# Modulation sums as rows, and latent heads scaled by token, in a two-block transformer kernel

## What is computed

```python
m_lat = silu(c) @ w_ada + b_ada            # 6 x 2048: sh1, sc1, g1, sh2, sc2, g2
m_ctx = silu(c_ctx) @ w_ada + b_ada        # only csh1, csc1 are used
u_lat = rmsnorm(x, norm1_g) * (1 + sc1) + sh1
u_ctx = rmsnorm(ctx, norm1_g) * (1 + csc1) + csh1
p_lat, p_ctx = u_lat @ w_in, u_ctx @ w_in
# HGRN2: 8 heads of 128, chunks of 64 tokens, in both directions
o = scores(q, k) @ v + (q * exp(a)) @ state             # 256 tokens x 128 per head
o = o * rsqrt(mean(o * o, axis=-1) + EPS) * norm_g      # mean over the head's 128 features
x = x + g1 * (concat(o * silu(g), hyena(p_lat)) @ w_out)
x = x + g2 * mlp(rmsnorm(x, norm2_g) * (1 + sc2) + sh2)
```

## Time and profile before

| | us |
|---|---|
| runs, median (lowest to highest of three) | 2680.01 (2679.8 to 2683.56) |
| the profiled execution's own time | 2679.24 |
| its span | 2677.4 |
| PE matmul busy | 2642.8 (99%) |
| DVE busy | 1833.4 (68%) |
| ACT busy | 1323.8 (49%) |
| POOL busy | 281.4 (11%) |
| HBM traffic over the span | 212 GB/s |

### The profile page before, as it was taken

One profiled execution on the slowest core, in us unless ns is written; L12 is line 12 of the kernel. 1 busy time (PEld: TensorE's weight loads), 2 busy tenths in 40 slices (PEclk: granted clock), 3 DMA queues, 4 the chain that ended last, 5 costly groups with the idle time before them and its releaser, 6 DMA issues.

```text
span 2677.4 us, 42752 instructions
## 1 busy us (share of the span) xinstructions
PE 2642.8 (99%) x18168; PEld 2414.4 (90%) x18168; DVE 1833.4 (68%) x2189; ACT 1323.8 (49%) x1746; POOL 281.4 (11%) x255
## 2 busy tenths in 40 slices
PE   9999999999999999999999999999999999999998
PEld 8888976998998989988999999998898898998997
DVE  5555665798999777787678866676555675445555
ACT  5455553554443443466874345666454444443443
POOL 1232321010000000010010311110000000000011
PEclk9999999999999999999999999999999999999999
DMA  9545454577777777795566744445657775555553
GB/s 308 171 156 158 146 175 143 195 262 269 271 260 285 269 284 282 283 338 176 157 233 243 266 134 150 136 151 194 219 170 251 266 282 196 190 177 196 188 179 124
DMA packets 289117, 571.28 MB, mean 213 GB/s; under 512 B 9702, under 2 KB 32513, under 8 KB 288608
## 3 DMA queue, kind: packets, MB, share of 16 engines
q1 hardware_dynamic: 283376, 548.69, 60.2%
q0 software_dynamic: 5552, 19.87, 2.5%
HBM read 564.73 MB, written 3.27 MB: 212 GB/s over the span
## 4 chain that ended last, share of the span: by engine, by line
PE 94%; DVE 3%; ACT 3%; issue 1%; POOL 0%; ACTq 0%; DVEq 0%; POOLq 0%
PE p_gemm L2110 49%; PE p_gemm L2159 32%; PE p_gemm L2136 3%; DVE w_lo L1232 1%; ACT w_hi L691 1%; PE p_b L2183 1%; PE p_b L2313 1%; PE p_b L2344 1%; PE p_b L2508 1%; PE p_b L2517 1%; PE p_b L2572 1%; PE p_b L2406 1%; PE p_gemm L2129 0%; PE p_b L2220 0%; PE p_b L2327 0%
## 5 line engine op out<-in xcount | busy, mean ns | idle before, releaser
L1232 DVE TENSOR_TENSOR w_lo<-w_raw,w_hi 128x1024 fp32r<-128x1024 f32 (+2 forms) x872 | 1068.5, 1229 | 729.7 <-ACT w_hi L691 728.5
L691 ACT ACTIVATE w_hi<-w_raw 128x1024 fp32r<-128x1024 f32 (+2 forms) x872 | 898.8, 1033 | 1226.4 <-PE p_gemm L2110 690.8
L2110 PE MATMUL p_gemm<-h_hi,w_hi 128*128 128x256 f32 x2928 | 831.5, 284 | 4.6 <-DVE w_lo L1232 2.5
L2110 PE MATMUL p_gemm<-h_lo,w_hi 128*128 128x256 f32 x2928 | 822.6, 281 | 0.0
L2110 PE MATMUL p_gemm<-h_hi,w_lo 128*128 128x256 f32 x2928 | 822.5, 281 | 0.0
L2110 PEld LDWEIGHTS p_gemm<-h_hi,w_hi 128*128 128x128 f32 x2928 | 551.7, 188 | 13.2 <-issue 7.1
L2110 PEld LDWEIGHTS p_gemm<-h_lo,w_hi 128*128 128x128 f32 x2928 | 551.9, 188 | 0.4
L2110 PEld LDWEIGHTS p_gemm<-h_hi,w_lo 128*128 128x128 f32 x2928 | 551.7, 188 | 0.0
L2159 PE MATMUL p_gemm<-w_hi,a_hi 128*128 128x512 f32 (+1 forms) x1056 | 406.1, 385 | 0.1
L2159 PE MATMUL p_gemm<-w_hi,a_lo 128*128 128x512 f32 (+1 forms) x1056 | 404.4, 383 | 0.0
L2159 PE MATMUL p_gemm<-w_lo,a_hi 128*128 128x512 f32 (+1 forms) x1056 | 404.2, 383 | 0.0
(11 more groups left out here) (402 smaller groups left out, 2483.2 us busy)
## 6 DMA issues: line engine op xcount, KB each, us to landing
w_raw<-in_w_mlp SPq DMA_DIRECT2D x124, 1024.0 KB, 5.2
w_raw<-in_w_in SPq DMA_DIRECT2D x107, 1024.0 KB, 5.3
ada_w<-in_w_ada SPq DMA_DIRECT2D x96, 1024.0 KB, 5.5
w_raw<-in_w_up SPq DMA_DIRECT2D x64, 1024.0 KB, 7.5
w_raw<-in_w_down SPq DMA_DIRECT2D x64, 1024.0 KB, 8.2
w_raw<-in_w_out SPq DMA_DIRECT2D x32, 1024.0 KB, 5.1
w_raw<-in_w_in SPq DMA_DIRECT2D x36, 768.0 KB, 4.7
cmp_w<-in_phi_w POOLq DMA_DIRECT2D x2, 2048.0 KB, 19.1
```

Of the source, the lines that this page charges most:

```text
L691: act.activation(WH[:, s % 4, :, 0:n], RAW[:, s // 2, 2 * (s % 2):2 * (s % 2) + 2, 0:n], ACT.Copy)\
L1232: dve.tensor_tensor(WL[:, s % 4, :, 0:n], RAW[:, s // 2, 2 * (s % 2):2 * (s % 2) + 2, 0:n], WH[:, s % 4, :, 0:n].bitcast(F32), ALU.subtrac ...
L2110: ins = pe.matmul(dst, w[:, s % 4, kk, cols], x[:, k, :], start=k == 0 and m % 2 == 0 and i == 0, stop=k == KC - 1 and i == 2, skip_group_ ...
```

## The change

It does four things.

1. The totals of the modulation become rows. ACT splits the sum's top off (`ada_top`, slot 0), DVE the rest (`ada_rest`, slot 1), and PE streams both, 512 columns of fp32r, against a weight with one column of ones (`SEL`), so that total i lands in row i of the bank; `ADA_AT` is 3 instead of 2. Three times (`MOD_AT`: blocks 33, 57, 75) DVE copies the rows out in slot 1, PE turns them behind unit 4, DVE adds the bias in slot 5. The last four totals, the gate g2, are broadcast to all rows by PE and added onto the bias rows on DVE (`gate_row`); `gain_rows` in the last MLP goes. ADA work starts in block 16, and no longer runs in block 55, so total 15 moves from block 56 to block 48.
2. The squares of the context move to slot 3 of blocks 36 to 39; its scalings and turns, and the latent tokens' turns, get other slots.
3. `lat_outputs` swaps weights and streaming operand: the output has tokens on the partitions, the eight state matmuls have 64 columns of weights and stream 128 columns. ACT's square sums by itself (`accum_out`), the ones-matmul goes, logarithm and exponential are of two elements a partition. DVE scales (`lat_scale`, slot 3), PE turns back (`lat_turn`, behind unit 4; for the last head behind unit 2 of block 71), DVE multiplies by the gain (`lat_out`, slot 5; slot 3 in block 71).
4. Around block 72 the gate's logarithm and exponential are parted, and the splits of slots 0 and 1 of block 72 move ahead of the exponential and behind the gating.

The core of the diff (the slot tables, ACT, DVE, PE):

```diff
-ADA_AT = 2
+ADA_AT = 3
-ADA_BLOCKS = [*range(17, 48), *range(55, 62), 72, 73, *range(80, 88)]
+ADA_BLOCKS = [*range(16, 48), *range(56, 62), 72, 73, *range(80, 88)]
-C_SCALE = (13, 15, 19, 22)
-C_TURN = (14, 15, 16, 17, 20, 21, 23, 24)
+C_SCALE = (0, 5, 11, 18)
+C_TURN = (1, 3, 7, 9, 13, 16, 20, 23)
-U_SCALE = (6, 11, 19, 29)
-U_TURN = (9, 14, 20, 25, 30, 36, 41, 46)
+U_SCALE = (6, 11, 19, 33)
+U_TURN = (12, 14, 20, 28, 36, 44, 52, 54)
...
+            def ada_top(b):
...
+                act.wait_ge(S("ada_summed"), 2 * UPB * (i + 1))
+                if i < ADA_CTX:
+                    act.activation(ADAT[:, 2, :], CTXA[:, i % 2, :], ACT.Copy)
+                act.activation(ADAT[:, 0, :], ADA[:, 1, 3, :], ACT.Copy).then_inc(S("ada_hi"), 1)
...
+            def ada_rest(b):
...
+                dve.wait_ge(S("ada_hi"), i + 1)
+                if i < ADA_CTX:
+                    dve.tensor_tensor(CTXL[:, i % 2, :], CTXA[:, i % 2, :], ADAT[:, 2, :].bitcast(F32), ALU.subtract)
+                dve.tensor_tensor(ADAT[:, 1, :], ADA[:, 1, 3, :], ADAT[:, 0, :].bitcast(F32), ALU.subtract).then_inc(S("ada_lo"), 1)
...
-                pe.wait_ge(S("ada_summed"), 2 * UPB * (i + 1))
-                if i < ADA_CTX:
-                    for m in range(4):
-                        col = 96 + 4 * i + m
-                        pe.matmul(PADA[:, col:col + 1], CTXA[:, i % 2, P * m:P * m + P], ONE[:, 0:1], start=True, stop=True)
+                pe.wait_ge(S("ada_lo"), i + 1)
+                halves = (ADAT[:, 0, :], ADAT[:, 1, :])
+                if i >= ADA_G2:
+                    ps = bank(i % 2, "mod_ready", i - ADA_G2 + 4)
+                    for n, w in enumerate(halves):
+                        ins = pe.matmul(ps[:, :], SEL[:, 31:32].to_broadcast([P, P]), w, start=n == 0, stop=n == 1)
+                else:
+                    rows = [(i if i < ADA_CTX else i + 8, halves)]
+                    if i < ADA_CTX:
+                        rows.append((i + 8, (ADAT[:, 2, :], CTXL[:, i % 2, :])))
+                    for row, ws in rows:
+                        for n, w in enumerate(ws):
+                            ins = pe.matmul(PADA[0:32, :], SEL[:, 31 - row:63 - row], w, start=i == 0 and row == 0 and n == 0, stop=True,
+                                            skip_group_check=True)
...
-                        pe.matmul(PB[1][:, P * i:P * i + P], HVN[:, i, :], SCT[:, z, i, :], start=first, stop=False, skip_group_check=True)
+                        pe.matmul(PB[1][:, P * i:P * i + P], SCT[:, z, i, :], HVN[:, i, :], start=z == 0 and i == 0, stop=False,
+                                  skip_group_check=True)
...
-                        ins = pe.matmul(PB[1][:, ts], state, QAQ[:, z, ts], start=False, stop=z == 1, skip_group_check=True)
+                        ins = pe.matmul(PB[1][rows, cols], QAQ[:, z, CHUNK * n:CHUNK * n + CHUNK], state, start=False, stop=True,
+                                        skip_group_check=True)
...
+            def lat_turn(h):
+
+                ps = bank(1, "hg_out", 2 * h + 2)
+                for tb in range(2):
+                    ins = pe.transpose(ps[:, P * tb:P * tb + P], ON[:, tb, :], IDN[:, :])
+                ins.then_inc(S("hg_oturned"), 1)
...
-                        if s == 0 and h > 0:
-                            lat_square_sum(h - 1)
+                        if s == 4 and h > 0:
+                            lat_turn(h - 1)
...
-                if s == 0:
-                    lat_square_sum(HG - 1)
+                if s == 2:
+                    lat_turn(HG - 1)
...
+            def lat_scale(h):
+
+                dve.wait_ge(S("hg_ors"), h + 1)
+                for tb in range(2):
+                    ins = dve.tensor_scalar(ON[:, tb, :], PB[1][:, P * tb:P * tb + P], HRS[:, tb:tb + 1], None, ALU.mult)
+                ins.then_inc(S("hg_out"), 1)
```

More of the change, by code:

```diff
@@ L254, in program @@
         CTXA = at("ada_ctx", A0 + 68 * K, [P, 2, 512])
+        CTXL = at("ada_ctx_lo", A0 + 68 * K, [P, 2, 512], F32R)
+        ADAT = at("ada_tops", 72 * K, [P, 3, 512], F32R)
+        SEL = at("row_select", A0 + 72 * K, [P, 64], F32R)
+        MODR = [at(f"mod_rows{i}", A0 + 68 * K if i == 0 else A0 if i == 1 else A0 + 64 * K, [32, 512]) for i in range(3)]
         CX = [at("ctx_x0", A0 + 64 * K, [P, 2, 512]), at("ctx_x1", A0 + 68 * K, [P, 2, 512])]
@@ L1240, in slot @@
                     lo(b + 1, g, s + SPLIT_LEAD - UPB)
-            def ada_step(b, s):
+            def ada_rest(b):
+                if b not in ADA_TOTAL:
+                    return
+                i = ADA_TOTAL[b]
+                dve.wait_ge(S("ada_hi"), i + 1)
+                if i < ADA_CTX:
+                    dve.tensor_tensor(CTXL[:, i % 2, :], CTXA[:, i % 2, :], ADAT[:, 2, :].bitcast(F32), ALU.subtract)
+                dve.tensor_tensor(ADAT[:, 1, :], ADA[:, 1, 3, :], ADAT[:, 0, :].bitcast(F32), ALU.subtract).then_inc(S("ada_lo"), 1)
+            def ada_step(b, s):
+                if s == 1:
+                    ada_rest(b)
+                if b in MOD_AT:
+                    part = MOD_AT.index(b)
+                    if s == 1:
+                        modulation_rows(part)
+                    if s == 5:
+                        modulation(part)
+                if b in ADA_TOTAL and ADA_TOTAL[b] >= ADA_G2 and s == 5:
+                    gate_row(ADA_TOTAL[b] - ADA_G2)
                 if b not in ADA_STEP:
@@ L1698, in modulation, with gate_row @@
                 dve.sem_inc(S("mod_ready"), 1)
+            def gate_row(m):
+                row = G2B[:, 512 * m:512 * m + 512]
+                dve.wait_ge(S("ada_used"), ADA_G2 + m + 1)
+                dve.wait_ge(S("final_rows_loaded"), 32)
+                dve.tensor_tensor(row, row, PB[m % 2][:, :], ALU.add).then_inc(S("mod_ready"), 1)
             for g in range(GROUPS):
@@ L1847, in _ @@
                     ada_step(B_HY + i, s)
-                    if i == 1 and s == 4:
-                        modulation(1)
                     r = UPB * i + s
@@ L1965, in _ @@
             clamp_gate(1)
+            slot(B_WOUT2, None, 0)
+            ada_step(B_WOUT2, 0)
             gated(1)
+            slot(B_WOUT2, None, 1)
+            ada_step(B_WOUT2, 1)
             mixed_lo(3)
@@ L1970, in _ @@
                 for s in range(UPB):
+                    if m == 0 and s < 2:
+                        continue
                     if b < B_MLP2 - 1 or s < UPB - 1:
@@ L1973, in _ @@
                     ada_step(b, s)
-                    if m == 3 and s == 0:
-                        modulation(2)
                 dve.wait_ge(S("unit_used"), count(b + 1, None, UPB))
@@ L2054, in _ @@
                             rest_mod(6, s + 3, u2_half(s + 3), HL, HH)
-                        if g == 2 and q == 0 and s == 4:
-                            modulation(3)
                         if s == 1 and 1 <= q <= 4:
@@ L2525, in _ @@
                         ada_total(b)
+                    if b == MOD_AT[1] and s == 4:
+                        modulation_turn(1)
                     r = UPB * (b - B_HY) + s
@@ L2618, in _ @@
                         ada_total(b)
+                    if b == MOD_AT[2] and s == 4:
+                        modulation_turn(2)
                     if s == 2:
```

201 lines of the change are left out of this document (111 added, 90 removed).

## The result

The median of eight runs is 2689.55 us (2687.28 to 2698.46), against 2682.57 us for eight runs of the kernel before: a ratio of 1.0032, interval 1.0021 to 1.0042. The forecast was 2689.0. That closeness flatters it: two terms of the sum were wrong by more than 6 us each, with opposite signs, as the traces and the run fill_wait show. The profiled execution of the new kernel took 2698.46 us and is the slowest of its eight; it is set against the profiled execution of before, 2679.24 us, so the traces have to account for 19.2 us and not for 7.

The account below looks back on a forecast made before the run. TensorE was taken to bound the kernel, with 94% of the chain. Terms of -23.6 and +32.6 us gave +9.0 on a profiled 2679.24 us, with the runs' median 0.8 above: 2689.0 us, forecast 2685.5 to 2693, range 2671 to 2699.

Parts of the forecast that it names:

- Totals: Modulation totals on TensorE: fp32r matmuls of 512 columns plus 0.35 us switching replace one-column matmuls; gain 7.3 us.
- Gate rows and turns of the sums: Last MLP's four groups of gain rows go, -3.6 us; three turns of the sums come, +1.8 us.
- Outputs of a head: Eight state matmuls with swapped operands run in pairs on array halves: -0.7 us a head, -5.6 for eight.
- The turn of a scaled head: Blocks 64 to 70: TensorE waits for VectorE's scaling behind two splits, unit 5 starts 2.6 us later; +18.2 us.
- The last head: Block 71's turn waits for scaling behind VectorE's late split, +7.1 us; the wait at block 72's split goes, -2.6.
- Total 15 at block 48: TensorE waits 4.6 us on VectorE's late subtraction, 2.5 of it lost there anyway; +2.1 us.
- Context heads: Latent turns and ADA work moved off heads with late keys in blocks 49 to 55: 4.5 us back, bounds 0 and 6.
- Clock: One fall at 1.7 us behind each of the two long waits, +3.4 us; none behind the seven short ones.
- rival D: Slower: the clock also falls in three head waits, +5 us, 2694; chance 0.22 together with rival C.
- Rival A: Faster: VectorE's scaling in slot 3 of blocks 64 to 70 is in time, 2672 us; chance 0.14 in full.

Follow-up runs that it names:

- fill_wait: Changed kernel with four unused ones-matmuls of 256 columns put ahead of each of the seven turns of scaled heads; 2683.2 us, 1.0008 of the kernel before.
- scale_first: Changed kernel with VectorE scaling the head ahead of slot 3's weight split, not behind it; 2667.45 us, 0.9946 of the kernel before.
- turn_u5: Changed kernel with TensorE's turn of a scaled head in blocks 64 to 70 behind unit 5, not unit 4; 2666.75 us, 0.9946 of the kernel before.
- old_u_turn: late_turns with the latent turns and fourth scaling of blocks 49 to 54 in their slots of before; 2655.6 us, 0.9899 of the kernel before.
- again: The changed kernel itself, unedited, timed and profiled once more; 2691.1 us, 1.0038 of the kernel before.
- late_turns: Changed kernel with all head turns behind unit 5, output op ahead of slot 5's split, total 15 behind unit 7 of block 48; 2651.6 us, 0.9888.
- unpaired: Changed kernel with a head's eight state matmuls ordered so that neighbours write the same half of the partitions; 2691.4 us, 1.0037 of the kernel before.
- b48_late: Changed kernel with total 15 taken behind unit 7 of block 48, not unit 3; 2684.55 us, 1.0011 of the kernel before.

## Why the prediction was right, and where it was not

1. **Totals** (predicted -7.3): -13.8. Eight fell by 1.79 - 0.93, sixteen by 0.90 - 0.47 (medians of all of them). The bound "14 us without switching cost" held. The step that failed is the 0.35 us for switching to a part of the array, taken from the earlier trace rows: with 32 columns of weights 0.03 us is left beyond two 512-column matmuls at 0.22. The four totals with full weights cost the same 0.47. The row I went by was of another form, 64 columns, two halves and eight records; for that form term 3 found nearly as much.
2. **Gate rows and turns of the sums** (-3.6, +1.8): four groups of 0.89 us went, three turns of 0.55 came, -3.6 and +1.7.
3. **Outputs of a head** (-5.6): 0.56 x 8 = 4.5, so -4.5. The pairing is as the earlier trace rows showed it, 0.11 us a pair. It saves 1.70 - 0.86 = 0.84 us a head, and 0.28 of that are lost around the pairs, where I had 0.15.
4. **The turn of a scaled head** (+18.2): 2.59 us of wait, 0.43 of transposes, 0.42 of ones-matmul gone: 2.60 x 7 = 18.2. Right in its sum and its cause, which scale_first and turn_u5 show: VectorE's queue, TensorE a slot too early. The place of the output op told when a scaling in the same slot would run.
5. **The last head** (+7.1): a wait of 7.1 us; VectorE's split starts at 1848.33 and the scaling at 1849.47, behind ScalarE's late split as in the earlier trace rows. The transposes and the ones-matmul nearly cancel beside it, +7.1. The gain at block 72 (-2.6) was 2.85.
6. **Total 15 at block 48** (+2.1): the wait was 4.4 us (4.6 predicted from the earlier trace rows), what went in return 1.9 rather than 2.5 us: +2.5. The wait that I allowed for in block 60 came too, 1.0 us, and was not in the sum.
7. **Context heads** (-4.5): -4.0 to -4.5 by old_u_turn for the turns' slots, and -0.6 more in block 55: up to -5.0. In the traces blocks 49 to 63 hold -5.7 with the totals that lie there.
8. **Clock** (+3.4): this is the second step that failed. I counted one fall for each of the two long waits and wrote of the short ones "none taken, 12 us at most", because the 2.6 us wait of the earlier trace rows had brought none. They brought 6.4 to 7.9 us in a usual execution, 11.2 in the profiled one. That was rival D, at larger size: I priced it at three falls, +5. The long waits were each followed by a fall, as forecast. In the first profile the fall cost about 1.7 us behind the last head's and 1.8 behind the one in block 48, which cost 0.9 in four of the seven profiles that have it.

The sum with the measured terms is near the measurement again: +9.0 - 6.5 (totals) + 1.1 (outputs) - 0.2 (block 72) + 0.4 (block 48) + 1.0 (block 60) - 0.5 (context heads) - 0.8 (clock at block 48, by those four profiles) + 6.4 (clock in the heads) = +9.9. The median of the change is 7.0 above its eight runs of before, that of again 10.4 above its fifteen. So the forecast, slower by a little, had the right sign for the reasons given, while its number is owed to two mistakes that nearly cancel. Rival A names the condition under which the change would have been faster, and its reading was right as well: with the scaling in time (scale_first) the kernel takes 2667; A's 2672 lacks the totals' other 6.5 us.

## What to carry to other kernels

A new step on a saturated engine that depends on a queue of another is priced by where that queue stands at that moment, not by the two operations: here 0.6 us of scaling and 0.4 of turning cost 28 us, and moving the consumer one unit later, or the producer ahead of one queued split, gave 22 of them back. The largest part of the rest was the last head's wait of 7.1 us, which went when late_turns moved that turn by three units. When reading the trace of before for this, find the instruction that stands in the slot that the new one will have, and compare its start with the unit that the consumer would run next. And a wait of TensorE is counted with the clock that may fall behind it: where a row shows a wait without a fall, that is one case, not the rule.

## What the runs showed of the hardware

The fall of TensorE's clock follows the same wait in some executions and places and not in others: seven of seven waits of 2.6 us in the first profile and its repetition, three of seven in unpaired, five of seven in b48_late, none for the 0.9 us that were left in fill_wait and none for the 0.4 in scale_first. Each cost 1.3 to 2.7 us. The early wait of 2.4 to 2.8 us on VectorE is in all twelve profiles, and in five of them a fall follows it; the waits of 4.4 us at block 48 and of 7.1 us at the last head were followed by one in every profile that has them, seven each. Matmuls on different halves of the array ran side by side even when the program put other matmuls of the first half between them; the order mattered by 0.47 us in 2.5, not by the 0.86 that strict neighbours would give. The Trainium skill (TensorEngine Tiling (Array Packing), Key Properties) says that a change of tiling mode drains the engine; with 32 columns of weights the traces leave 0.03 us for it. With 64 in two halves 0.1 us is seen ahead of the first pair (the step from the last score matmul at 1603.65 to the first state matmul at 1603.86, less the usual 0.11), and 0.28 us in all, the 0.84 us that the pairs save less the 0.56 measured. That is a third of what the pairing saves, so it lessened the gain of this change and didn't undo it; that the 0.28 us are a drain is not shown.
